# Sums of squares with the tokens on partitions: root and reciprocal of 116x9 numbers, laid along all rows by small products

## The reference

```
def _rmsnorm(x, g):
    y = x32 * lax.rsqrt(jnp.mean(x32 * x32, axis=-1, keepdims=True) + NORM_EPS) * g

for l in range(DEPTH):
    u = _rmsnorm(h, norm_mix_pre[l])
    mix, v_first = _mixer(u, ...)          # one projection in; sparse attention and RWKV-7; one out
    h = h + _rmsnorm(mix, norm_mix_post[l])
    u = _rmsnorm(h, norm_ffn_pre[l])
    f = jnp.square(jax.nn.relu(u @ w_up[l])) @ w_down[l]
    h = h + _rmsnorm(f, norm_ffn_post[l])
```

## Time and profile before

| | |
|---|---|
| time, median of 3 | 4056.33 us (4054.54 to 4059.51) |
| the profiled execution's own time | 4055.09 us |
| its span, first to last instruction | 4053.3 us |
| mean granted TensorE clock | 0.945 of full speed |
| TensorE matmuls busy | 3724.1 us, 92% |
| weight loads busy | 2835.8 us, 70% |
| VectorE busy | 2177.3 us, 54% |
| ScalarE busy | 863.4 us, 21% |
| GpSimd busy | 556.3 us, 14% |

### The profile page before, as it was taken

One profiled execution on the slowest core, in us unless ns is written; L12 is line 12 of the kernel. 1 busy time (PEld: TensorE's weight loads), 2 busy tenths in 40 slices (PEclk: granted clock), 3 DMA queues, 4 the chain that ended last, 5 costly groups with the idle time before them and its releaser, 6 DMA issues.

```text
span 4053.3 us, 68954 instructions
## 1 busy us (share of the span) xinstructions
PE 3724.1 (92%) x29136; PEld 2835.8 (70%) x29136; DVE 2177.3 (54%) x4110; ACT 863.4 (21%) x1734; POOL 556.3 (14%) x444
## 2 busy tenths in 40 slices
PE   7999986999979999999889998869999799999995
PEld 4566564996548888888655665549956488888884
DVE  2599745776164243434646997467751632434345
ACT  1345562332010000000013445623320100000000
POOL 0041100000012222222100410000000122222220
PEclk9999995999889999999999999879989899999998
DMA  2001100000111111112210110100002111111121
GB/s 113 27 26 37 50 17 6 4 4 26 68 58 42 42 42 42 43 51 85 71 50 21 32 37 22 40 1 4 4 25 73 54 51 43 42 42 42 42 84 53
DMA packets 43384, 163.68 MB, mean 40 GB/s; under 512 B 5056, under 2 KB 5072, under 8 KB 42720
## 3 DMA queue, kind: packets, MB, share of 16 engines
q1 hardware_dynamic: 27648, 100.68, 7.3%
q0 software_dynamic: 15456, 58.85, 4.0%
HBM read 135.07 MB, written 23.49 MB: 39 GB/s over the span
## 4 chain that ended last, share of the span: by engine, by line
PE 77%; DVE 16%; issue 3%; ACT 2%; POOL 1%; DMA 0%; DVEq 0%; ACTq 0%; POOLq 0%
PE ps L713 38%; PE ps L739 10%; PE ps L662 9%; PE ps L630 6%; DVE arena L1454 4%; PE ps L922 2%; PE ps L910 2%; PE ps L964 1%; DVE little L1484 1%; PE ps L935 1%; PE ps L674 1%; PE ps L640 1%; DVE arena L1351 1%; DVE arena L1358 1%; ACT arena L1238 1%
## 5 line engine op out<-in xcount | busy, mean ns | idle before, releaser
L713 PE MATMUL ps<-arena 128*128 128x261 f32 x4096 | 924.7, 383 | 5.7 <-POOL arena L549 2.9
L713 PEld LDWEIGHTS ps<-arena 128*128 128x128 f32 x4096 | 775.1, 189 | 135.1 <-issue 5.4
L662 PE MATMUL ps<-arena,ring 128*128 128x348 f32 x2304 | 705.1, 465 | 36.4 <-DVE arena L1330 18.9
L713 PE MATMUL ps<-arena,ring 128*128 128x261 f32 x3072 | 706.2, 385 | 21.3 <-DVE arena L1828 21.0
L713 PEld LDWEIGHTS ps<-arena,ring 128*128 128x128 f32 x3072 | 585.0, 191 | 122.3 <-issue 21.5
L662 PEld LDWEIGHTS ps<-arena,ring 128*128 128x128 f32 x2304 | 439.3, 193 | 300.9 <-issue 59.8
L739 PE MATMUL ps<-arena 64*64 64x64 f32 (+1 forms) x13600 | 476.7, 225 | 70.9 <-DVE arena L1535 43.3
L739 PEld LDWEIGHTS ps<-arena 64*64 64x64 f32 x13600 | 452.1, 136 | 91.6 <-issue 45.5
L1309 ACT ACTIVATE aux<-ps 128x522 f32<-128x522 f32 x64 | 38.8, 607 | 1535.0 <-PE ps L713 1535.0
L1396 DVE TENSOR_TENSOR arena<-aux,ps 128x522 f32<-128x522 f32 x160 | 111.8, 699 | 426.7 <-PE ps L713 426.2
L549 POOL TENSOR_TENSOR arena<-ring 128x512 f32<-128x512 f32 x128 | 172.1, 1344 | 1106.8 <-DMA ring<-units 1101.4
(11 more groups left out here) (228 smaller groups left out, 3669.2 us busy)
## 6 DMA issues: line engine op xcount, KB each, us to landing
ring<-units SPq DMA_DIRECT2D x192, 512.0 KB, 3.7
h_scratch<-arena POOLq DMA_DIRECT2D x24, 522.0 KB, 3.2
arena<-h_scratch POOLq DMA_DIRECT2D x24, 522.0 KB, 7.9
arena<-h_in POOLq DMA_DIRECT2D x16, 522.0 KB, 10.9
out<-arena POOLq DMA_DIRECT2D x8, 522.0 KB, 3.2
arena<-att_scratch POOLq DMA_DIRECT2D x2, 2080.0 KB, 9.1
att_scratch<-arena POOLq DMA_DIRECT2D x16, 256.0 KB, 3.0
aux<-rope POOLq DMA_DIRECT2D x2, 1044.0 KB, 12.4
```

The source lines that it names most:

```text
L662: ins = mm(ps[:, b + s, 0:SW], ring[:, r * D + k * P:r * D + (k + 1) * P], tile(U0, k)[:, slice_(s)], start=(k == 0), stop=(k == KT - 1))
L713: ins = mm(acc_at(n)[:, s], lhs[:, k * P:(k + 1) * P], rhs(k)[:, s * HALF:(s + 1) * HALF], start=(k == 0), stop=(k == KT // 2 - 1))
```

## The change

The squares become the stationary operand and a single column of ones the moving one: a block of 116 tokens comes out on 116 partitions, one number each. Nine blocks (NTB = 9, TB = 116) make a tile; each of them, for each of the eight tiles, writes a column of its own in PSUM bank 7, with no accumulation. For eight tiles VectorE adds the eight columns of each block by a `tensor_reduce` into `norm_cols`, 116x9; ScalarE takes the root of these (of one tile, straight from PSUM) and VectorE the reciprocal. Then `norm_spread` on TensorE lays them along all 128 rows: nine products with the column, broadcast to 128, as the stationary operand and a 116x116 identity as the moving one write 128x1044 into three banks, which the scaling instructions read in place of `rstd`.

```
-            def norm_sums(count, sq, b=0):
+            def norm_sums(count, sq):
                 for k in range(count):
                     pe.wait_ge(S["sq_ready"], w.next("sq_ready"))
-                    for s in range(SLICES):
-                        ins = mm(ps[:, b + s, 0:SW], const("ones"), sq[k % 2][:, slice_(s)],
-                                 start=(k == 0), stop=(k == count - 1))
+                    for t in range(NTB):
+                        ins = mm(ps[0:TB, 7, count * t + k:count * t + k + 1], sq[k % 2][:, t * TB:(t + 1) * TB],
+                                 const("ones")[:, 0:1], start=True, stop=True)
                     ins.then_inc(S["sq_used"], 1)
+
+            def norm_spread(b):
+
+                pe.wait_ge(S["inverse_ready"], w.next("inverse_ready"))
+                for t in range(NTB):
+                    ins = mm(ps[:, b + t // 3, t % 3 * TB:(t % 3 + 1) * TB],
+                             norm_cols[:, t:t + 1].broadcast_to([TB, P]), ident[0:TB, 0:TB], start=True, stop=True)
+                ins.then_inc(S["inverse_spread"], 1)
...
-            def root(n, b=0):
-
-                act.wait_ge(S["sq_used"], w.value("sq_used", 2))
-                go(thirds(rstd), banks(b), ACT.Sqrt, bias=eps_norm, scale=1.0 / n).then_inc(S["root_ready"], 1)
+            def root(n, summed=False):
+
+                if summed:
+                    act.wait_ge(S["sums_added"], w.next("sums_added"))
+                else:
+                    act.wait_ge(S["sq_used"], w.value("sq_used", 2))
+                go(norm_cols, norm_cols if summed else ps[0:TB, 7, 0:NTB], ACT.Sqrt, bias=eps_norm[0:TB], scale=1.0 / n)\
+                    .then_inc(S["root_ready"], 1)
...
+            def inverse_root():
+                dve.wait_ge(S["root_ready"], w.next("root_ready"))
+                v.reciprocal(norm_cols, norm_cols).then_inc(S["inverse_ready"], 1)
+                dve.wait_ge(S["inverse_spread"], w.next("inverse_spread"))
+
+            def added_root():
+
+                w.skip("sq_used", KT)
+                dve.wait_ge(S["sq_used"], w.value("sq_used"))
+                v.tensor_reduce(norm_cols, ps[0:TB, 7, 0:KT * NTB].rearrange("p (t k) -> p t k", k=KT), AXIS, ALU.add)\
+                    .then_inc(S["sums_added"], 1)
+                inverse_root()
...
-                    v.scalar_tensor_tensor(tile(U0, k), h_at(k), par(l, gain, k), rstd, ALU.mult, ALU.mult)\
+                    v.scalar_tensor_tensor(thirds(tile(U0, k)), thirds(h_at(k)), par(l, gain, k), banks(SLICES), ALU.mult, ALU.mult)\
```

More of the change, by code:

```diff
@@ L26 @@
 ACT = mybir.ActivationFunctionType
+AXIS = mybir.AxisListType.X
 P = 128
@@ L104 @@
 TAIL0 = SC0 + sum(SEL_W[FIRST_SEL:])
+NTB, TB = 9, W // 9
 SPLIT, HALF = W // 2, W // 4
@@ L268, in trunk @@
         little = sb("little", 8 * NSEL + 4 * NQB + 20 + 4 + len(SIGNED))
+        norm_cols = sb("norm_cols", NTB)[0:TB, :]
         sel, wi = little[:, 0:7 * NSEL], little[:, 7 * NSEL:7 * NSEL + 4 * NQB]
@@ L284, in trunk @@
             "tile_out", "z_ready",
-            "sq_ready", "sq_used", "root_ready", "u_ready", "h_ready", "mix_ready",
+            "sq_ready", "sq_used", "root_ready", "sums_added", "inverse_ready", "inverse_spread", "u_ready", "h_ready", "mix_ready",
             "products", "acc_free", "first_out", "sums_ready", "weights_ready",
@@ L344, in trunk @@
         stage = arena[:, TAIL0:TAIL0 + W]
-        rstd = arena[:, SQ0 + 2 * W:SQ0 + 3 * W]
         junk = [arena[:, TAIL0 + 1048 + 264 * j:TAIL0 + 1048 + 264 * (j + 1)].bitcast(U8) for j in range(3)]
@@ L828, in _ @@
                 norm_sums(KT, sq_at)
+                norm_spread(SLICES)
                 unit(l, 0)
@@ L1041, in _ @@
                 norm_sums(1, [sq_sum])
+                norm_spread(0)
                 norm_sums(KT, sq_at)
+                norm_spread(4)
                 for q in range(2 * SQUARES):
@@ L1058, in _, with squares @@
                 w.skip(name, n)
-            def root(n, b=0):
-                act.wait_ge(S["sq_used"], w.value("sq_used", 2))
-                go(thirds(rstd), banks(b), ACT.Sqrt, bias=eps_norm, scale=1.0 / n).then_inc(S["root_ready"], 1)
-            def squares(count, src, sq, n, b=0, ready=False, landed=False):
+            def root(n, summed=False):
[5 more added lines that the diff above has]
+                    .then_inc(S["root_ready"], 1)
+            def squares(count, src, sq, n, ready=False, landed=False):
                 for k in range(count):
@@ L1074, in squares @@
                     go(sq[k % 2], src(k), ACT.Square).then_inc(S["sq_ready"], 1)
-                root(n, b)
+                root(n, summed=True)
             def copies(count, dst, func=ACT.Copy, group=1):
@@ L1318, in _ @@
                 nc.vector.sem_inc(S[name], n)
-            w = Tally(dve, S, tile_out=2, s_out=2, y_out=1, kk_out=2)
+            w = Tally(dve, S, tile_out=2, s_out=2, y_out=1, kk_out=2, sq_used=2)
             def do(ins):
@@ L1323, in do @@
                 dve.wait_ge(S["dve_done"], w.next("dve_done"))
+            def inverse_root():
[8 more added lines that the diff above has]
+                inverse_root()
             def normed(l, gain):
-                dve.wait_ge(S["root_ready"], w.next("root_ready"))
-                do(v.reciprocal(rstd, rstd))
+                added_root()
                 for k in range(KT):
-                    v.scalar_tensor_tensor(tile(U0, k), h_at(k), par(l, gain, k), rstd, ALU.mult, ALU.mult)\
+                    v.scalar_tensor_tensor(thirds(tile(U0, k)), thirds(h_at(k)), par(l, gain, k), banks(SLICES), ALU.mult, ALU.mult)\
                         .then_inc(S["u_ready"], 1)
@@ L1344, in add_normed @@
             def add_normed(l, src, gain, res):
-                dve.wait_ge(S["root_ready"], w.next("root_ready"))
-                do(v.reciprocal(rstd, rstd))
+                w.skip("sq_used", 1)
+                inverse_root()
                 scaled = []
@@ L1350, in add_normed @@
                     if k < KT:
-                        v.scalar_tensor_tensor(src(k), src(k), par(l, gain, k), rstd, ALU.mult, ALU.mult)\
+                        v.scalar_tensor_tensor(thirds(src(k)), thirds(src(k)), par(l, gain, k), banks(0), ALU.mult, ALU.mult)\
                             .then_inc(S["dve_done"], 1)
@@ L1824, in _ @@
                 add_normed(l, mix_at, "mix_post", h_at)
-                dve.wait_ge(S["root_ready"], w.next("root_ready"))
-                do(v.reciprocal(rstd, rstd))
+                added_root()
                 for k in range(KT):
-                    v.scalar_tensor_tensor(tile(U0, k), h_at(k), par(l, "ffn_pre", k), rstd, ALU.mult, ALU.mult)\
+                    v.scalar_tensor_tensor(thirds(tile(U0, k)), thirds(h_at(k)), par(l, "ffn_pre", k), banks(4), ALU.mult,
+                                           ALU.mult)\
                         .then_inc(S["u_ready"], 1)
```

## The result

| | before | after |
|---|---|---|
| median, 20 runs each | 4065.44 us (4053.2 to 4071.9) | 4072.49 us (4063.2 to 4082.08) |
| ratio of the times | | 1.0024, 95% interval 1.0014 to 1.0033 |
| profiled execution, its own time | 4055.09 us | 4073.88 us |
| its span | 4053.3 us | 4071.7 us |

The changed kernel is slower, by 0.24% or 9.8 us in the ratio of the runs: little, but clear of the noise, since the interval leaves out 1. A second comparison with 5 runs of it gave 1.0039 (1.0025 to 1.0053), so the two together lie near 0.3%. Between the two profiled executions the difference is larger, 18.4 us; the median of before in 20 runs lies 10 us above its profiled execution. That gap is taken up with the experiments.

The account below looks back on a forecast made before the run. The prediction took matmuls on TensorE (busy 92%) to bound the kernel, with engines working in turn around the norms. Its terms, 9.9 + 25.2 - 10.3 = +24.8 us on 4055.1, gave 4079.9, or 4081 for the median; range 4062 to 4100.

Parts of the forecast that it names:

- Sums at the low clock throughout: In the long norms TensorE's new sums run at 1.2 GHz from first to last, 3.6 us a tile.
- Pitch of a load: In the new sums, each load of 116 stationary columns with one moving column costs 0.20 us at 1.2 GHz.
- Tail of a long norm: From last sum to first scaled tile (reduction, root, reciprocal, spread): 5.3 us instead of 8.0.
- Long norms: Mix-pre and ffn-pre norms, summing eight tiles: +9.9 us in layer 0's mix-pre, +8.4 us in each of the other three.
- Short norms: Mix-post and ffn-post norms, with one summed tile: -2.6, -2.4, -2.9 and -2.4 us, together -10.3 us.
- Sum: All eight norms together: 9.9 + 25.2 - 10.3 = +24.8 us on the profiled execution's 4055.1 us.
- the sooner clock of the first unit: Line 662's first unit, behind the spread, could save up to 2.9 us in each of two places; counted as nothing.
- narrow sums that warm the clock: Rival: the clock rises some 4.5 to 6 us into a long norm; total -35 us, 4021 us; chance 0.07.
- loads at full speed at the low clock: Rival: in sums and spreads a load takes 0.104 us even at 1.2 GHz; total -31 us, 4025 us; chance 0.05.
- loads without overlap: Rival: each narrow record in sums and spreads pays its whole load, 0.338 us; +110 us on the forecast, 4191 us; chance 0.05.

## Why the prediction was right, and where its size was off

- *Sums at the low clock throughout*: right, in all four long norms of both traces. That gapless work of 64 rows hadn't raised the clock was the row that told it. The reason, one column per load, was right only in part: the clock stayed low behind 64 columns too (0.194 us a record), and came up behind 128, with the same loads.
- *Pitch of a load*: 0.194 us measured, 0.20 forecast. The slope of 1.67 ns a column was right (116 x 1.67 = 0.193), the 0.007 us gap taken from the warm loads was not there. Sums of a long norm 28.0 us instead of 29.15.
- *Tail of a long norm*: 5.06 measured, 5.3 forecast, with reduction 0.23, root 0.30, reciprocal 0.21 and spread 4.04 (forecast 0.22, 0.18, 0.20, 4.4). The root came out above its bound of 0.28, at no cost that matters.
- *Long norms*: +8.6 (forecast +9.9), and +7.1, +6.9, +7.2 (forecast +8.4 each): +29.8 for +35.1.
- *Short norms*: -2.3, -2.8, -3.3, -3.0 (forecast -2.6, -2.4, -2.9, -2.4): -11.4 for -10.3.
- *Sum*: +18.4 in the two traces for +24.8. The mis-sized term is that of the sums: four times 1.15 us of the 6.4; the rest is the tails, 4 x 0.25 of the long and 1.1 us of the short norms, less rounding.
- *In the runs* it is +9.8 us, below half of the forecast: the forecast took the difference of two executions for that of the medians, on a median of 3 runs of before at 4056.3 that 20 runs put at 4065.4. The execution profiled was a quick one by the clock at the start of layer 1's chunk loop; and the 3 to 9 us by which the ratios put the changed kernel better than its norms were in no term of the sum (the sooner clock of the first unit was kept for the lower end, with 5.8 us). That 4072.5 lies only 8.5 us under the 4081 forecast is in part luck: a start some 9 us too low and a difference 15 us too large offset each other.
- *The rivals*: narrow sums that warm the clock, loads at full speed at the low clock, and loads without overlap are all refuted by 0.194 us at 0.50: the first by the clock, the second (0.104) and the third (0.338) by the pitch. The Trainium skill's rule in "TensorE: Matmul & The Clock Gate", section "LDWEIGHTS (loading the stationary operand)", P / 1.2 without the clock, gives an estimate of 97 ns for 116 columns. No run here agrees at the low clock (194 ns); at the high one a pitch of 108 ns was measured, with 128 columns behind each load.

## What to carry to other kernels

Before a reduction on TensorE is turned round so that the data become the stationary operand, count the records and look at the clock that they will run at: here a load followed by one column took 0.194 us, a load followed by 128 took 0.212 at the low clock, and behind the latter the clock came up and the record fell to 0.108. Where TensorE waits and narrow work follows, products of constants into an unused bank cost nothing in the two places where they were tried, and the next stage was faster. And compare many executions, or stage by stage in the traces: two spans alone were off by a factor of two here.

## What was not expected

- With 128 columns streamed behind each load the clock rose from 0.50 to 1.00 some 5.4 us into three of the long norms and 3.6 us into the first; with 64 columns, loads at the pitch of the single column, it stayed at 0.50 for 28 us. The faster kernel does more work in its sums: 4025.8 against 4072.5 us.
- 28 records of constants in an idle stretch of each layer of the unchanged kernel make it 0.3 to 0.5% faster (0.9971 and 0.9954), of which the stage behind them shows 4.3 us.
- One step ahead of the chunk loop takes 48.1 or 56.7 us in layer 0 and 71.1 or 81.0 in layer 1, by how long the clock stays up in it, and one and the same kernel meets both.
- The first unit behind the spread ran in 15.8 us in both layers in one execution of the changed kernel and in 17.9 and 18.7 in another: which level of the clock it gets differs between executions.
